# Unit 1 of a hybrid attention and state-space layer as three fp32r products, unit 2's weights in a third raw buffer, and VectorE's output maps in units 4 to 7

## What is computed

```python
xn = rmsnorm(h, norm1_g)
proj = xn @ w_in                                  # 1024 -> q, k, v, u, gates
q, k, v, u, gates = jnp.split(proj, [...], axis=-1)
attn = stick_breaking_attention(rmsnorm(q), rmsnorm(k), v)
y = s5_ssm(u, ...)                                # complex diagonal states, 32 groups of 16 channels
g = gelu(y); ssm = g * sigmoid(g @ w_glu + b_glu)
h = h + (sigmoid(gate_a) * (attn @ w_attn_proj) + sigmoid(gate_s) * (ssm @ w_ssm_proj)) @ w_o
up = causal_dwconv(rmsnorm(h, norm2_g) @ w_up)
h = h + (silu(gate_f) * val_f) @ w_down
```

## Time and profile before

| | us |
|---|---|
| median of 3 runs | 706.69 |
| the three runs | 706.46, 706.69, 709.88 |
| profiled execution, its own time | 707.04 |
| span of its profile | 705.3 |
| busy: PE, PEld, DVE, ACT, POOL | 694.5, 662.4, 422.4, 322.0, 184.3 |

### The profile page before, as it was taken

How to read it: one execution, slowest core, us unless ns; L and a number is a source line. 1 busy time by engine, 2 the same in 40 slices (tenths; PEclk the granted TensorE clock), 3 DMA queues, 4 the chain that set the end, 5 groups by cost and what they waited for, 6 DMA issues and landing times.

```text
span 705.3 us, 14227 instructions
## 1 busy us (share of the span) xinstructions
PE 694.5 (98%) x5680; PEld 662.4 (94%) x5680; DVE 422.4 (60%) x559; ACT 322.0 (46%) x483; POOL 184.3 (26%) x209
## 2 busy tenths in 40 slices
PE   9999989989999999999999999999999999999998
PEld 7899979989999999999999999999999998888887
DVE  5775989687777756445766666666666662322221
ACT  4754543668889653445444444444343432111220
POOL 7899999920000023231101010101101010000000
PEclk9999999999999999999999999999999999999999
DMA  8168344249211234333333333333333342333331
GB/s 232 47 186 135 78 124 135 64 139 114 70 60 53 68 91 121 90 91 90 90 91 90 89 89 89 91 91 99 98 96 90 100 124 82 98 97 97 97 98 46
DMA packets 139930, 69.26 MB, mean 98 GB/s; under 512 B 23476, under 2 KB 137880, under 8 KB 139888
## 3 DMA queue, kind: packets, MB, share of 16 engines
q1 hardware_dynamic: 139727, 68.65, 36.7%
q10 hardware_dynamic: 160, 0.02, 0.0%
HBM read 63.19 MB, written 4.28 MB: 96 GB/s over the span
## 4 chain that ended last, share of the span: by engine, by line
PE 90%; DVE 4%; ACT 2%; issue 2%; SPq 1%; DMA 1%; POOL 0%; DVEq 0%; ACTq 0%; POOLq 0%
PE ps L1814 80%; PE ps L1841 1%; PE ps L2017 1%; PE ps L2067 1%; PE ps L1865 1%; DVE lo L1309 1%; PE ps L1970 1%; PE ps L2034 1%; ACT xh L994 1%; PE ps L1961 1%; DVE mod L500 1%; SPq L540 1%; DVE gates L499 1%; DVE gates L501 1%; PE ps L1874 1%
## 5 line engine op out<-in xcount | busy, mean ns | idle before, releaser
L925 ACT ACTIVATE hi<-raw 128x1024 fp32r<-128x1024 f32 (+2 forms) x102 | 111.5, 1094 | 244.2 <-PE ps L1814 226.6
L1814 PE MATMUL ps<-xh,hi 128*128 128x264 f32 (+1 forms) x1088 | 219.5, 283 | 0.1
L1814 PE MATMUL ps<-xl,hi 128*128 128x264 f32 (+1 forms) x1088 | 218.7, 282 | 0.0
L1309 DVE TENSOR_TENSOR lo<-raw,hi 128x1024 fp32r<-128x1024 f32 (+2 forms) x102 | 135.5, 1328 | 138.9 <-ACT hi L925 138.3
L1814 PE MATMUL ps<-xh,lo 128*128 128x264 f32 (+1 forms) x1088 | 218.0, 282 | 0.0
L1814 PEld LDWEIGHTS ps<-xh,hi 128*128 128x128 f32 x1088 | 167.3, 189 | 1.5 <-issue 0.6
L1814 PEld LDWEIGHTS ps<-xl,hi 128*128 128x128 f32 x1088 | 166.8, 188 | 0.0
L1814 PEld LDWEIGHTS ps<-xh,lo 128*128 128x128 f32 x1088 | 166.6, 188 | 0.0
L908 POOL TENSOR_TENSOR cv<-cv 128x512 f32<-128x512 f32 x22 | 28.3, 1289 | 226.7 <-DVE cv L1766 226.7
L1814 PE MATMUL ps<-ah,hi 128*128 128x512 f32 (+1 forms) x198 | 74.3, 375 | 0.0
L1814 PE MATMUL ps<-al,hi 128*128 128x512 f32 (+1 forms) x198 | 73.1, 369 | 0.0
(11 more groups left out here) (298 smaller groups left out, 956.0 us busy)
## 6 DMA issues: line engine op xcount, KB each, us to landing
raw<-in_w_up_dram SPq DMA_DIRECT2D x88, 256.0 KB, 3.1
raw<-in_w_in_dram SPq DMA_DIRECT2D x52, 256.0 KB, 3.4
raw<-in_w_down_dram SPq DMA_DIRECT2D x16, 384.0 KB, 3.5
raw<-in_w_down_dram SPq DMA_DIRECT2D x16, 320.0 KB, 4.0
raw<-in_w_o_dram SPq DMA_DIRECT2D x16, 256.0 KB, 3.0
xtok<-in_x_dram SPq DMA_DIRECT2D x4, 512.0 KB, 5.5
raw<-in_w_ssm_proj_dram SPq DMA_DIRECT2D x8, 256.0 KB, 2.8
out_dram<-yt SPq DMA_DIRECT2D x7, 256.0 KB, 2.4
```

What stands on the lines that cost most here:

```text
L925: act.activation(hi[slot][:, 0:n * P], raw[slot][:, 0:n * P], ACT.Copy)\
L1309: dve.tensor_tensor(lo[slot][:, 0:n * P], raw[slot][:, 0:n * P], hi[slot][:, 0:n * P].bitcast(F32), ALU.subtract)\
L1814: ins = pe.matmul(o, weights[w], acts(a, c), start=start and i == 0, stop=stop and i == 2)
```

## The change

It does five things.

1. Unit 1 becomes a split unit (`U_PLAIN = 1`). ACT rounds its weights before the second half of the transposed tokens is copied; GpSimd, which scales only unit 0's weights now, makes the low part and signals `lo_first`. PE's unit 1 takes the tiles of `xh` and `xl` one by one as they get ready.
2. DVE makes `xh` of tiles 0 and 1 itself (`XH_HERE`), ACT the other six.
3. Unit 2's weights go to a third buffer, `raw_third`, loaded right behind unit 1's; ACT and DVE split them right after `xh` and `xl`, before unit 0's and 1's results are brought out. SP's loads of units 3 and 4 wait for `lo_first` and unit 0.
4. DVE's output maps stand behind units 4, 5, 6 and 7 and are four: half 0 of rounds 0, 1 and 2, and half 1 of round 2. Their scratch is `raw_third`. GpSimd makes half 1 of rounds 0 and 1 and all of round 3. DVE's part of `norms` (now `rates`) goes from unit 9 to behind `turn_v` of unit 10.
5. GpSimd's last list, `hT` times `rb`, stops after four of eight until the last `state` is done. `rms_set` and the skip terms move to behind unit 3.

The core of the diff:

```diff
-U_PLAIN = 2
+U_PLAIN = 1
+XH_HERE = 2
...
-         3: [("turns", 0)], 4: [("columns", 1), ("turns", 1)],
-         5: [("square", 0)], 6: [("square", 1), ("out_map", 0)],
-         7: [("square", 2), ("out_map", 1)], 8: [("square", 3), ("out_map", 2), ("prep", 0)],
+         3: [("turns", 0), ("early_rows", 0)], 4: [("columns", 1), ("turns", 1), ("out_map", 0)],
+         5: [("square", 0), ("out_map", 1)], 6: [("square", 1), ("out_map", 2)],
+         7: [("square", 2), ("out_map", 3)], 8: [("square", 3), ("prep", 0)],
          9: [("state", 0), ("norms", 0)],
-         10: [("prep", 1), ("turn_v", 0)], 11: [("readout", 0), ("state", 1)],
+         10: [("prep", 1), ("turn_v", 0), ("rates", 0)], 11: [("readout", 0), ("state", 1)],
...
+MAPS_HERE = ((0, 0), (1, 0), (2, 0), (2, 1))
+MAPS_THERE = {0: (1,), 1: (1,), 3: (0, 1)}
+DVE_MAPS, POOL_MAPS = (1, 2, 4, 4), (1, 2, 2, 3)
...
             load(1, source(1))
+            load_into(raw_third, third_in, source(2))
...
-                if done < U_PLAIN:
-                    sp.wait_ge(unit_done, done + 1)
-                else:
+                if done == 1:
+                    sp.wait_ge(lo_first, 1)
+                elif done == 2:
+                    sp.wait_ge(unit_done, 1)
+                elif done:
                     sp.wait_ge(lo_ready, done + 1)
-                load((done + 2) % 2, source(done + 2))
+                if done:
+                    load((done + 2) % 2, source(done + 2))
...
             plain_weights(0)
-            plain_weights(1)
...
+            pool.wait_ge(hi_ready, 2)
+            pool.tensor_tensor(lo[1][:, 0:KD * P], raw[1][:, 0:KD * P],
+                               hi[1][:, 0:KD * P].bitcast(F32), ALU.subtract).then_inc(lo_first, 1)
...
             output_map(1)
             input_map(1)
-            output_map(2)
             input_map(2)
             input_map(3)
-            output_map(3, (0, 1))
+            output_map(3)
...
             for k in range(KD):
+                if k == KD // 2:
+                    pool.wait_ge(st_set, ROUNDS)
                 pool.tensor_tensor(hT[:, k, :], hT[:, k, :], rb[:], ALU.mult).then_inc(h_raw, 1)
...
             token_scale(1, 3)
+            act.nop().then_inc(hi_ready, U_PLAIN)
+            split(1, 1, KD)
             turned_x(1)
...
-            for k in range(KD):
+            for k in range(XH_HERE, KD):
                 act.activation(xh[:, k], hT[:, k], ACT.Copy, scale=g1[:, k:k + 1])\
                     .then_inc(xh_set, 1)
+            split_third()
...
+                if k < XH_HERE:
+                    link(dve.tensor_scalar(xh[:, k], hT[:, k], g1[:, k:k + 1], None, ALU.mult))
+                else:
+                    dve.wait_ge(xh_set, k - XH_HERE + 1)
...
+            dve.wait_ge(lo_first, 1)
+            dve.nop().then_inc(lo_ready, U_PLAIN + 1)
...
-            for c in range(2):
-                plain_half(1, c)
-
...
-                pe.wait_ge(lo_ready, unit + 1)
-                if unit != U_GLU + 1:
+                if unit == U_PLAIN:
+                    pe.wait_ge(lo_first, 1)
+                else:
+                    pe.wait_ge(lo_ready, unit + 1)
+                if unit >= 2 and unit != U_GLU + 1:
                     pe.wait_ge(*left(unit - 2))
```

More of the change, by code:

```diff
@@ L226, in hybrid_trunk @@
         pad = alloc(mix, "pad", [P, 4 * (L - LL)])
+        maps = ExitStack()
+        raw_third = alloc(maps, "raw_third", [P, KD * P])
+        map_tmp = raw_third[:, 0:RP * (T8 + 1) * GH]
+        maps.close()
         v2 = alloc(mix, "v2", [P, 5, HEADS, 2 * DH], F32R)
@@ L323, in hybrid_trunk @@
         lo_ready = sem("lo_ready")
+        third_in = sem("third_in")
+        lo_first = sem("lo_first")
         unit_done = sem("unit_done")
@@ L549, in in_cols, with load_into @@
                 return w_in[0].rearrange("(k p) c -> p k c", p=P)[:, :, c0:c0 + P]
-            def load(slot, parts):
+            def load_into(tile, landed, parts):
                 at = 0
@@ L555, in load @@
                     n = src.shape[1] * src.shape[2]
-                    sp.dma_start(raw[slot][:, at:at + n].rearrange("p (k c) -> p k c", c=src.shape[2]),
-                                 src).then_inc(raw_in[slot], 16)
+                    sp.dma_start(tile[:, at:at + n].rearrange("p (k c) -> p k c", c=src.shape[2]),
+                                 src).then_inc(landed, 16)
                     at += n
+            def load(slot, parts):
+                load_into(raw[slot], raw_in[slot], parts)
             def halved(src):
@@ L835, in input_map, with output_map @@
                 pool.nop().then_inc(g_ready, 1)
-            def output_map(r, parts=(1,)):
+            def output_map(r):
                 if r >= HOUTS:
                     pool.wait_ge(y_ps, r - HOUTS + 1)
-                for c in parts:
+                for c in MAPS_THERE[r]:
                     map_part(pool, link, r, c, pt, RP if r < 2 else RP // 2)
@@ L920, in split @@
             def split(unit, slot, n):
-                act.wait_ge(raw_in[slot], (unit - slot) * 16 + 32)
+                act.wait_ge(raw_in[slot], (unit - slot) * 16 + 32 * slot)
                 if not isinstance(unit, int) or unit >= 2:
@@ L926, in split, with split_third @@
                     .then_inc(hi_ready, 1)
+            def split_third():
+                act.wait_ge(third_in, 32)
+                act.activation(hi[0][:, 0:KD * P], raw_third[:], ACT.Copy).then_inc(hi_ready, 1)
             act.preload_act_table_set("natural_log_exp_and_others")
@@ L1197, in _ @@
                     evacuate(unit)
-                split(unit + 2, unit % 2, tiles_of(unit + 2))
+                if unit:
+                    split(unit + 2, unit % 2, tiles_of(unit + 2))
                 if unit >= U_HEADS:
@@ L1308, in split @@
                 dve.wait_ge(hi_ready, unit + 1)
-                dve.tensor_tensor(lo[slot][:, 0:n * P], raw[slot][:, 0:n * P],
+                src = raw_third if isinstance(unit, int) and unit == 2 else raw[slot]
+                dve.tensor_tensor(lo[slot][:, 0:n * P], src[:, 0:n * P],
                                   hi[slot][:, 0:n * P].bitcast(F32), ALU.subtract)\
@@ L1465, in angle, with early_rows @@
                        .then_inc(ang_set, 1)
+            def early_rows(_):
+                dve.tensor_tensor(rt[:, 3], rt[:, 1], rt[:, 2], ALU.mult).then_inc(rms_set, 1)
+                dve.tensor_tensor(skip_i[:], ident[0:GH, 0:GH].unsqueeze(1)
+                                  .broadcast_to([GH, GROUPS, GH]),
+                                  colc[0:GH, ROW_SKIP:ROW_SKIP + GROUPS].unsqueeze(2)
+                                  .broadcast_to([GH, GROUPS, GH]), ALU.mult)
             def turns(i):
@@ L1487, in columns, with rates @@
                 ins.then_inc(ct_set, 1)
-            def norms(_):
+            def rates(_):
                 dve.wait_ge(rs_a, 1)
@@ L1671, in evacuate @@
                 dve.tensor_copy(*unit_tile(unit)).then_inc(gate_late, 1)
-            steps = {"columns": columns, "out_map": out_map, "angle": angle, "turns": turns,
-                     "norms": norms, "scale": scale, "prep": prep, "state": state,
+            steps = {"early_rows": early_rows, "columns": columns, "out_map": out_map, "angle": angle, "turns": turns,
+                     "rates": rates, "scale": scale, "prep": prep, "state": state,
                      "head": head,
```

27 lines of the change are left out of this document (8 added, 19 removed).

## The result

The changed kernel takes 711.1 us (median of 18 executions, 709.46 to 712.26) against 706.91 for the kernel before (18, 706.22 to 712.23) on the same chip. The ratio is 1.0045, 95% interval 1.0033 to 1.0057: slower by 0.45%. The medians themselves lie 4.2 us or 0.59% apart; the ratio is not one of medians and is the smaller figure. So the change is slower by 3 to 4 us, about the 0.5% by which two executions differ, while the forecast was 703.8 and its range ended at 706.6. The profiled execution took 710.04 us with a span of 708.3, against 705.3 before: 3.0 us more, where the sum had 2.9 less.

What follows compares the result with a forecast made beforehand. The prediction took TensorE's own work (98% of the span) and two waits ahead of `readout` as the bound. Balances of +2.2, -4.4, +0.4 and -1.1 us gave -2.9, from 706.69 to 703.8 us, range 700.6 to 706.6.

Steps and rivals of the forecast that it cites:

- the sum: Whole kernel: the terms added up to 2.9 us less, span 705.3 to 702.4 us.
- Unit 1: Start: split unit 1 takes 5.9 us instead of 7.34, ends at 31.6, gains 1.4 us.
- The low part on GpSimd: Start: GpSimd makes unit 1's low part in about 2.8 us, done by 22.4, wanted at 25.7.
- The maps: Units 4 to 7: maps of 5.2 us cause gaps of 2.1 and 1.5 us at units 7 and 8; unit 9 2.2 late.
- the rival on the clock: Units 7 and 8: clock falls in the early gaps, costing 1.5 us behind unit 8's; 705.3 us, chance 0.15.
- The first `readout`: Round 0: v ready at about 100.9, TensorE at 101.7; the 2.9 us gap and slow clock (1.5) go, 4.4 us.
- The second `readout`: Round 1: norms behind v put the last tap at 119.5, TensorE comes at 119.1; gap 0.4, 0 to 1.5.
- The last `readout`: Round 3: `state` 3 alone takes 5.8 us instead of 7.6, taps are late next; gain 1.1 us, 0.7 to 1.7.
- The head gives nothing: Rival at the start: unit 2 waits for its low part, starts at 33.06 as before; 705.2 us, chance 0.12.
- the slower case: Rival: map and low part take over 8.1 us per unit, the gap moves and deepens; 708.5 us, chance 0.08.

Runs made afterwards that it cites:

- e2: Changed kernel with unit 1's low part made by VectorE behind its copies of `hT`, none of it on GpSimd: 707.88 us, ratio 1.0009 to the kernel before.
- e1: Changed kernel with GpSimd making unit 1's low part only after VectorE's small operations on the angles: 708.07 us, ratio 1.0006 to the kernel before.
- e3: Changed kernel with the taps of round 1 ahead of the norms' read on SyncE's queue: 708.09 us, ratio 1.0013 to the kernel before.
- e4: Changed kernel without the stop in GpSimd's last list, all eight multiplications in a row: 712.48 us, ratio 1.0083 to the kernel before.
- e5: Changed kernel with the edits of e2 and e3 together: 705.44 us, ratio 0.9972 to the kernel before.
- e7: Kernel before with the new start alone (unit 1 split, third raw buffer, unit 1's low part on VectorE): 707.74 us, ratio 0.9995.
- e8: e5 with GpSimd's eight multiplications behind unit 20 and VectorE's three maps behind units 6 to 8, as before: 713.33 us, ratio 1.0078 to the kernel before.
- e9: e8 with the skip term (`prep` 0) ahead of the third map and GpSimd's eight multiplications in two fours: 708.60 us, ratio 1.0017 to the kernel before.
- e10: Kernel before with `prep` 0 ahead of the third map, norms behind `turn_v` of unit 10, taps 1 ahead of the norms' read: 707.88 us, ratio 0.9992.
- e12: Changed kernel with the edits of e2 and e3, first map behind unit 3, taps 3 behind unit 18's load: 699.59 us, ratio 0.9890 to the kernel before.
- e11: e9 with the taps of round 3 behind the load of unit 18 on SyncE's queue: 706.86 us, ratio 0.9978 to the kernel before.

## Why the prediction was wrong

By its own steps, in the profiled executions. "Forecast" and "was" are TensorE's time against before:

| place | forecast | was | error that is new there |
|---|---|---|---|
| unit 2 | -1.5 | +2.3 | 3.8 |
| unit 9 | +2.2 | +5.9 | -0.1 |
| unit 12 | -2.2 | +1.4 | -0.1 |
| unit 14, behind `readout` 1 | -1.8 | +3.7 | 1.9 |
| unit 17, behind `readout` 3 | -2.9 | +2.0 | -0.6 |
| behind the first `suffix`, and the end | -2.9 | +3.0 | 1.0 |

**Unit 1: the first step that failed.** The gain of 1.4 us itself is real (e2: unit 2 at 31.3). "The low part on GpSimd" was costed by its own 2.8 us (it took 2.35) and by when it was wanted, and not by whom it shuts out. Its neighbours on VectorE were small and looked cheap, and behind them stood the copies of `hT` that TensorE waits for. The prediction quoted the Trainium skill's rule on just this (SBUF — State Buffer, Who interferes with whom) and applied it to the maps alone. The trace agrees with the rule at the head too: a `SCALAR_TENSOR_TENSOR` on 128x16 elements took 2.29 us beside GpSimd's 2.35, and 0.17 without. The lateness cost 2.2 us, and e1 and e2 show its cause. The slower clock of the plain half cost 1.45 more against the forecast's 3.67; it belongs to this execution (e3 and e4 have the wait without it), and what makes it stays open.

**The maps: right.** 5.17 and 2.02 us for 5.2 and 2.0, unit 9 later by exactly the 3.6 us of its step. Unit 8 had no gap of its own: unit 7 ran at 1.2 GHz for part of its time and ended at 75.25, when unit 8's low part, ready at 75.18, was there. The slower clock filled the gap that was forecast and cost nothing, as the rival on the clock said of unit 7. With unit 7 at full clock (e2 to e5) both gaps are there, 2.4 to 2.5 and 1.3 us.

**The first `readout`: right, with a part of the reason too large.** -4.4 forecast, -4.5 measured. With the start put right (e2) its times hold one by one: the skip term at 86.0, v at 101.1 (forecast 100.9), TensorE at 101.8 (101.7). The prediction let the norms bring v forward by 1.4 us; e7 and e8 show 0.8 at most, since v's high part, behind SyncE's chain, comes at 100.7 to 100.9 in both. Most of the wait went because TensorE came later, which the sum did count, and which is no gain: e9 and e10, with the skip term ahead of the third map, have no gaps at units 7 and 8 and start `readout` 0 behind 0.7 us and without a wait (e10 with a start that was 2.3 us late).

**The second `readout`: the second step that failed.** The chain was followed from the norms to the taps of round 1 and from there to TensorE. That it also goes through ScalarE was missed: the copy of the taps of round 2 waits for `kern` to be moved out, and v stands behind it in ScalarE's stream. The time of the taps was also off (issued to 120.7, landing near 122, forecast 119.5), since the norms ended later with everything else. That lateness is not the cause: in e2 the last tap is issued at 117.4, as forecast (117.5), ScalarE's copy starts at 118.64, v is there at 121.5, and the gap is 2.3. Gap 2.2 instead of 0.4; e3 shows that it is the queue's order.

**The last `readout`: right, but for the stop.** 1.7 us gained for a forecast of 1.1, `state` 3 took 5.8 us as forecast, and the wait is now for taps, as said. Whether the stop was needed for `state` 3 could be seen in the list's times: with half a round of maps less, GpSimd starts its last list 6 us earlier, would be through at 141.9 (e4), and `state` 3 starts at 145.9. The stop guards `state` 2 instead (e4: 1.5 us in the trace, 2.7 by the ratios).

**Behind it: not in the sum.** Unit 18's weights behind the taps of round 3 cost 1.0 us. The order was the same before; it cost nothing there, because the taps were issued 3.7 us earlier. e12 against e5 shows it with 1.0 us in the trace, e11 against e9 with 0.5.

**Of the rivals** two came near. The clock fell at unit 7 as that rival had it, but not behind unit 8, where its 1.5 us were to be lost; the 1.45 us came in the start. "The head gives nothing" named the right place with the wrong mechanism (unit 2 waiting for its low part, which it never did) and had unit 2 at its old time, not 2.3 us later. The range ended at 706.6, and only the slower case (0.08) lay beyond it, because no case had the head as a loss.

## What to carry to other kernels

Price an instruction that is moved to GpSimd by what VectorE does in those microseconds, down to its smallest two-operand instructions, and by what stands behind these. A step that overwrites a small staging tile (`kern`) ties the engine that fills it to the queue that empties it; follow that edge as well as the one to the consumer. When a wait disappears, look whether its cause moved or TensorE only came later: e7 and e8, which undo parts of the change, put the wait back in full, and only moving the cause (the skip term ahead of a map, a map into idle time, the taps ahead of a read) made the kernel faster.
